# Attention of a hybrid decoder layer on one core: all tokens ahead of the expert gather, or the second half of the tokens between its slots

## Time and profile before

| | us |
|---|---|
| median of 3 runs | 3849.35 (3846.76 to 3849.93) |
| the profiled execution | 3843.72 |
| its span, first to last instruction | 3841.9 |
| mean granted TensorE clock | 0.953 |
| first slot's product (DVE, line 1436) starts | 1045.9 |
| last slot's product starts | 3825.2 |

### The profile page before, as it was taken

One profiled execution on the slowest core, in us unless ns is written; L12 is line 12 of the kernel. 1 busy time (PEld: TensorE's weight loads), 2 busy tenths in 40 slices (PEclk: granted clock), 3 DMA queues, 4 the chain that ended last, 5 costly groups with the idle time before them and its releaser, 6 DMA issues.

```text
span 3841.9 us, 34099 instructions
## 1 busy us (share of the span) xinstructions
PE 3173.3 (83%) x9592; PEld 1711.9 (45%) x9592; DVE 2383.7 (62%) x5856; ACT 1312.8 (34%) x3737; POOL 1447.5 (38%) x1288
## 2 busy tenths in 40 slices
PE   7888886698899799978897889998777777777776
PEld 5767665577444355534443444443222222222222
DVE  4555555314366687767766676666666667667664
ACT  2333333322133345543333233333333333333332
POOL 2122210241044456545544344333444444344442
PEclk9989896899899999999998999999999999999999
DMA  2000000521599999999999899999999999999997
GB/s 84 17 23 22 22 11 4 226 75 65 186 409 421 418 393 413 420 407 408 406 388 398 337 387 420 420 421 421 417 420 416 414 415 417 416 413 414 418 418 328
DMA packets 190464, 1203.34 MB, mean 313 GB/s; under 512 B 21840, under 2 KB 30032, under 8 KB 58704
## 3 DMA queue, kind: packets, MB, share of 16 engines
q0 software_dynamic: 147456, 1073.81, 68.1%
q1 hardware_dynamic: 42112, 127.43, 8.9%
q10 hardware_dynamic: 720, 0.13, 0.0%
HBM read 1180.31 MB, written 20.97 MB: 313 GB/s over the span
## 4 chain that ended last, share of the span: by engine, by line
DMA 28%; PE 23%; DVE 7%; ACT 3%; issue 3%; POOL 1%; POOLq 0%; DVEq 0%
DMA ring<-uv,idx 27%; PE r_o L1600 18%; DVE ring L1436 5%; PE w_ps L1475 3%; PE w_ps L1586 1%; ACT diag L1128 1%; ACT gel L1118 1%; ACT coef L1122 0%; POOL ring L953 0%; ACT L1103 0%; DMA y_scr<-zn 0%; DVE wo L1244 0%; DVE gates L1240 0%; PE w_ps L1569 0%; DVE yn_e L1414 0%
## 5 line engine op out<-in xcount | busy, mean ns | idle before, releaser
L1600 PE MATMUL r_o<-ring,diag 128*128 128x512 f32 x4096 | 1958.6, 613 | 456.7 <-ACT diag L1128 456.2
L953 POOL DMA_INDIRECT ring<-uv,idx x1024 | 1147.7, 1121 | 1614.0 <-PE r_o L1600 1513.6
L1436 DVE CUSTOM_DVE_ANT_0 ring<-ring,ytok 128x1024 f32<-128x1024 f32 x1024 | 1295.3, 1266 | 681.4 <-DMA ring<-uv,idx 680.3
L1600 PEld LDWEIGHTS r_o<-ring,diag 128*128 128x128 f32 x4096 | 762.4, 193 | 1463.5 <-ACT diag L1128 730.8
L1118 ACT ACTIVATE gel<-dot 128x2 f32<-128x2 f32 x512 | 104.1, 203 | 1695.6 <-DVE dot L1436 1694.7
L1128 ACT ACTIVATE diag<-ident,coef 128x128 f32<-128x128 f32 x1024 | 348.0, 387 | 3.2 <-PE r_o L1600 3.1
L1475 PE MATMUL w_ps<-xh,wb 128*128 128x512 f32 x640 | 270.9, 473 | 37.6 <-POOL wb L926 37.2
L67 PE MATMUL j_ps<-xT_hi,wa 128*128 128x512 f32 x768 | 258.6, 409 | 18.6 <-DVE xT_lo L355 18.6
L1586 PE MATMUL w_ps<-yT,wq 128*128 128x512 f32 x512 | 257.0, 604 | 5.2 <-DMA wq<-wq 4.5
L1122 ACT ACTIVATE coef<-gel,gate 128x1 f32<-128x1 f32 x1024 | 245.9, 287 | 16.8
L250 POOL TENSOR_SCALAR st_a<-st_a 128x1 f32<-128x1 f32 x64 | 12.2, 191 | 489.5 <-ACT sq L305 489.5
(11 more groups left out here) (162 smaller groups left out, 3014.5 us busy)
## 6 DMA issues: line engine op xcount, KB each, us to landing
wb_raw<-w_in SPq DMA_DIRECT2D x40, 512.0 KB, 7.7
wq<-wq SPq DMA_DIRECT2D x32, 512.0 KB, 7.9
ring<-uv,idx POOLq DMA_INDIRECT x1024, 13.0
wa_raw<-w_in SPq DMA_DIRECT2D x24, 512.0 KB, 3.3
wc_raw<-w_branch SPq DMA_DIRECT2D x16, 768.0 KB, 8.6
wo_raw<-w_out SPq DMA_DIRECT2D x16, 512.0 KB, 15.7
s_scr<-s_out SPq DMA_DIRECT2D x16, 512.0 KB, 9.6
s<-s_scr SPq DMA_DIRECT2D x64, 128.0 KB, 10.3
```

Source lines behind the costliest of these rows:

```text
L953: nc.gpsimd.indirect_dma_start(out=ring[t % RING][:], out_offset=None, in_=a["uv"], in_offset=bass.IndirectOffsetOnAxis(ap=idx[:, slot:slo ...
L1436: nc.vector.tensor_tensor_reduce(ring[r][:, 0:D], ring[r][:, 0:D], ytok[n % 2][:], 1.0, 0.0, ALU.mult, ALU.add, dot[:, slot:slot + 1]).the ...
L1600: ins = nc.tensor.matmul(o_ps[n % 2][half][:], diag[t % DIAGS][:], ring[t % RING][:, D + half * HALF:D + (half + 1) * HALF], start=slot == ...
```

## The change

Both blocks become one, `build`. Everything now runs by halves of the tokens, attention included.

- Half 0 (`stage(0)`, `BASES[0] = -4000`): 44 units (4 pooling, 8 each of q, k and v, 16 gates) of 512 tokens as before in three float32r matmuls, then 32 attention steps in plain float32. k and v of this half are stored in DRAM (`k_scr`, `v_scr`).
- Half 1 (`stage(1)`, `BASES[1] = 57`): 44 units, 32 attention steps against the keys of both halves, branch products and `w_out`, all in plain float32 and with no split. The gates of this half are stored in `g_scr` as they are made and loaded again after the attention. k and v of half 0 come back per head.
- In the gather nothing changes. `by_vector` always returns False, so `PE_SUMS[t]` is `t + 1`.

The slot numbers, and the order on each engine within `stage(g)`:

```diff
-BASES = (-4000, 72)
-UNIT_LEN = 6; BRANCH_LEN = 13; NORM_LEN = 12; HEAD_LEN = 16
+SEQ = [("p", i) for i in range(NP)] + [(r, 0) for r in "qkv"]
+for _h in range(H):
+    SEQ += ([(r, _h + 1) for r in "qkv"] if _h + 1 < H else []) + [("g", 2 * _h), ("g", 2 * _h + 1)]
+BASES = (-4000, 57)
+LAND = 12
+STEP = 6
+NSTEP = H * GT
+T_U = LAND
+T_A = T_U + 4 * (NP + 3) + 2
+T_B, BRANCH_LEN = T_A + 205, 9
+T_N, NORM_LEN = T_B + BRANCH_LEN * DC + 3, 12
+HEAD_LEN = (14, 16)
+SCORES_AT = (-69, 443)
+DO_LOGIT = (1, 1)
+DO_EXP = (3, 5)
+DO_MIX = (5, 6)
+DO_TURN = (8, 7)
+DO_VALUES = (11, 11)
+DO_OSB = (12, 12)
+DO_SQUARE = (13, 13)
+DO_ROOT = (15, 15)
+DO_ON = (17, 17)
+DO_OT = (22, 22)
+def unit_at(g, i):
+    if i < NP + 3:
+        return BASES[g] + T_U + 4 * i
+    i -= NP + 3
+    head, j = (i // 5, i % 5) if i < 5 * (H - 1) else (H - 1, i - 5 * (H - 1) + 5)
+    return BASES[g] + T_A + GT * STEP * head + (0, 4, 8, 14, 18, 2, 6)[j]
+def step_at(g, k):
+    return BASES[g] + T_A + STEP * k
+def merged(*streams):
...
+        head = min(live, key=lambda item: item[0])
+        yield head[0]
+        head[0] = next(head[1], None)
```

`stage(g)` is now `merged(...)` of separate streams; of equal slot numbers the earlier stream goes first. On PE the streams are units, pooling, scores, turns, values, outs, rest:

```diff
+        def units(g):
...
+                for c in range(DC):
+                    yield unit_at(g, i) + c // 3
...
+                        ins = nc.tensor.matmul(bank[:], w_raw[1][i % 3][:, c, :], x_raw[1][:, c, :], start=c == 0,
+                                               stop=c == DC - 1)
+        def scores(g):
...
+                for c in range(g + 1):
+                    yield step_at(g, k) + 2 * c
...
+                    if i >= 2:
+                        pe.wait_ge(logit_done, i)
+                    source = k_own[g][h % 2] if c == g else k_old[h % 2]
+                    for wh in range(2):
+                        rows = slice(wh * DH, (wh + 1) * DH)
+                        nc.tensor.matmul(score_bank(g, wh)[:, 0:n], q[g][h % 2][rows, qs], source[rows, 0:n], start=True,
+                                         stop=True).then_inc(s_ready, 1)
+        def turns(g):
...
+                    yield step_at(g, k) + DO_TURN[g] + 2 * c
+        def values(g):
...
+                yield step_at(g, k) + DO_VALUES[g]
+        def outs(g):
...
+                yield step_at(g, k) + DO_OT[g]
```

On DVE (streams pooling, logits, outputs, transposed, rest), and the exponentials on ACT:

```diff
+        def logits(g):
...
+                for c in range(g + 1):
...
+                    for wh in range(2):
...
+                        yield step_at(g, k) + DO_LOGIT[g] + (2 * c + wh if g else 0)
...
+                        dve.wait_ge(s_ready, i + 1)
...
+                yield step_at(g, k) + DO_MIX[g]
...
+                dve.wait_ge(e_ready, 2 * m + 2)
+        def outputs(g):
...
+                yield step_at(g, k) + DO_OSB[g]
+                dve.wait_ge(o_done, m + 1)
...
+        def transposed(g):
...
+                yield step_at(g, k) + DO_OT[g] + 1
+                dve.wait_ge(on_turned, m + 1)
...
+        def exponents(g):
...
+                yield step_at(g, k) + DO_EXP[g]
+                act.wait_ge(mx_ready, m + 1)
+                for wh in range(2):
+                    nc.scalar.activation(e[g][k % 2][:, wh, 0:n], e[g][k % 2][:, wh, 0:n], ACT.Exp,
+                                         bias=nmx[:, wh:wh + 1], accum_out=den[:, wh:wh + 1]).then_inc(e_ready, 1)
```

More of the change, by code:

```diff
@@ L43 @@
 KB = 1024
[L46 to L53, removed]
-BASE = 16512
[L59 to L70, removed]
@@ L76 @@
[L76 to L97, removed]
@@ L100 @@
[L100 to L117, removed]
@@ L812, in stage @@
[L812 to L820 removed]
+                for c in range(2):
+                    load_branch(0, c)
+                sp.dma_start(gb[:, 0], a["ln2_g"].to_broadcast([P, D])).then_inc(gb_in, 16)
@@ new lines, in rest @@
+            sp.wait_ge(unit, UNITS * (g + 1))
+            if g:
+                for r in range(2):
+                    sp.wait_ge(gate_saved[r], 16 * NGATE // 2)
+                for half in range(2):
+                    sp.dma_start(gates[1][:, DC * half:DC * (half + 1)],
+                                 g_scr[DC * half:DC * (half + 1)].rearrange("j p w -> p j w")).then_inc(gate_back, 16)
+                load_branch(1, 1)
+                yield step_at(g, NSTEP - 1) + DO_ON[g] + 2
+                sp.wait_ge(on_ready, NSTEP * (g + 1))
@@ L821, in stage @@
+            load_out(g)
             for n in range(2, DC):
@@ L867, in stage @@
             store_scores(RH - 1)
+        def stage(g):
+            if g == 0:
+                return merged(units(0), keys_out(), rest(0))
+            return merged(rest(1), units(1), gate_stores(), keys_back())
         def search_in(k):
@@ L938, in stage @@
                 nc.gpsimd.tensor_tensor(rstd1, var1, mhalf1, ALU.pow).then_inc(rstd1_ready, 1)
+        def stage(g):
+            if g == 0:
+                return merged(units(0), roots(0), rest(0))
+            return merged(roots(1), rest(1))
         def root(n):
@@ L1034, in stage @@
[L1034 to L1042 removed]
+                yield unit_at(g, i) + 3
+                act.wait_ge(unit, UNITS * g + i + 1)
@@ L1054, in turned @@
+                nc.scalar.activation(mt_of(n)[0][:], gates[0][:, 0:DC, n * P:(n + 1) * P], ACT.Copy).then_inc(m_hi, 1)
             def turned(n):
@@ new lines, in units, with pooling @@
+                ins.then_inc(unit, 1)
+                if SEQ[i][0] == "v":
+                    yield unit_at(g, i) + 4
+                    pe.wait_ge(evac, u + 1)
+                    if i == NP + 2 and g == 0:
+                        pe.wait_ge(consts, 5)
+                    for b in range(GT):
+                        ins = nc.tensor.transpose(bank[:, b * P:(b + 1) * P], vT[g][:, b * P:(b + 1) * P], ident[:])
+                    ins.then_inc(v_turned, 1)
+        def pooling(g):
+            for i in range(NP):
+                b = NP * g + i
+                yield unit_at(g, i) + (7 if g else 9)
+                bank = ps[2 + b % 2]
@@ new lines, in outs @@
+        def outs(g):
+            for k in range(NSTEP):
+                m = NSTEP * g + k
+                yield step_at(g, k) + DO_OT[g]
+                pe.wait_ge(on_ready, m + 1)
+                if g == 0 and k:
+                    pe.wait_ge(o_ready, m)
+                if g:
+                    behind = min(k + 3, NSTEP - 1)
+                    pe.wait_ge(logit_done, score_no(1, behind, 1, 1) + 1)
+                nc.tensor.transpose(out_bank(g)[:, 0:P], on[:], ident[:]).then_inc(on_turned, 1)
@@ L1590, in stage @@
                         compare(hp - 1)
-            yield score_at(g, RH) + 8
+            yield score_at(g, RH) + part
             compare(HP * (g + 1) - 1)
+        def stage(g):
+            return merged(units(g), pooling(g), scores(g), turns(g), values(g), outs(g), rest(g))
         def spread(n, slot):
             t = SLOTS * n + slot
-            pe.wait_ge(diag_ready, t + 1)
+            u = PE_SUMS[t]
+            pe.wait_ge(diag_ready, u)
             if slot == 0 and n >= 2:
```

1384 lines of the change are left out of this document (663 added, 721 removed).

## The result

The changed kernel takes **4101.6 us** (median of 4, 4094.0 to 4104.4) against 3848.1 of the kernel before on the same chip (4 runs, 3845.1 to 3849.9): ratio **1.0656, 95% interval 1.0638 to 1.0675**. It is slower, as forecast, but by 254 us instead of 117, and outside the range. The execution profiled took 4094.0 us (span 4092.2), 0.2% under the median.

A forecast was written before the change was run, and what follows sets the result against it. PE, busy 83% of the span, was held to stand waiting for diagonals when DVE waits between slots. 566 to the first product + 2314 outside the steps + 1084 in them = 3964, 3966 with the surround; range 3860 to 4060.

The forecast's parts named there:

- Three VectorE waits a step: Steps, slots 99 to 291: DVE waits for PE at one slot's distance three times a step, for logits twice and the copy.
- the clock: Steps: after a wait PE runs at the lower clock level; 1.2 us for each of 32 steps, 38 us.
- Part 2: Gather slots outside the steps, with half 1's units, branch and norm between them, plus the end: 2314 us.
- The new DMA traffic: Gather: some 24 MB more, 57 us at 420 GB/s, costs nothing because slots 69 to 376 take over 2.9 us.
- The forecast's own sign of being wrong: Wrong if slots 99 to 291 take under 5 us each, or the first product is later than 620 us.
- Part 1: Ahead of the gather: half 0's attention, branch at 353 us, first product at 566 us instead of 1046, -480.
- the forecast's lower bound for the first product: Ahead of the gather: first product at 535 us if PE runs without gaps.
- Part 3: The 32 steps among slots 99 to 291: 1084 us, 5.6 a slot; bounds 706 and 1150.
- The scores: Steps: score matmuls of 64 rows run side by side, 0.86 us a pair of 512 columns; other bound 1.72.
- The mechanism's fine print: Steps: each DVE wait stands ahead of a pair's second product, so PE stands for the rest of the round.
- The first rival: Steps: PE is the bound and the waits are covered, 706 instead of 1084 us, total 3588; chance 12%.
- Its condition: Steps: the result is faster than before once they need under about 955 us.

The follow-up runs named there:

- e11: Single-slot kernel (GROUP 1, 3826 us) with first three weight blocks loaded earlier and GpSimd's first two branch splits earlier: 8 us less; first product 630.5 against 628.0.
- e10: Changed kernel, pairs kept, VectorE's waits for TensorE and the mix in second-half steps at two slots, transposed output in the values' bank: 3725 us.
- e1: Changed kernel with the second half's stage begun one slot later (BASES 58 for 57), shifting step parity against the pairs: 29 us less.
- e12: The two-slot kernel with pairs (3725 us), only the logits put back to one slot behind their scores: +163 us.
- e14: The two-slot kernel with pairs (3725 us), only the mix put back to one slot behind the exponentials: +66 us.
- e15: The two-slot kernel with pairs (3725 us), only the copy of the transposed output put back to one slot behind its transpose: +55 us.
- e2: Changed kernel with ScalarE making gel, coefficient and diagonal slot by slot instead of in pairs (GROUP 1 for 2): 3826 us, 276 us less.
- e3: Changed kernel with the gather's Gelu replaced by Exp (output differs), removing 73 of 105 table loads in the steps' stretch: 26 us less.

## Why the prediction was right and wrong

**Right: the sign and its reason.** The gain ahead of the gather is given away in the steps, because VectorE waits inside its queue of products and TensorE then stands for diagonals. Three VectorE waits a step, the clock after them, slots 443 on at the old rates: as forecast. Part 2 was forecast at 2314 us with its end and took 2311 (4092.2 - 629.6 - 1151.6). That it fits to 3 us is in part luck: the branch took 16 more and the norm tiles 17 less than forecast. The new DMA traffic cost nothing visible: slots 57 to 99 took 141 us for 145 forecast.

**Wrong: two terms, 64 and 68 us.** Less the 3 us of part 2 they make the 128 us by which the profiled execution (4094.0) missed the forecast; the median lies another 8 above it. The forecast's own sign of being wrong, a first product later than 620 us, came up; the other, under 5 us a slot in the steps, did not (6.0).

*Part 1, the first product at 566 us; it was 629.6.* The step that failed is the 334 us from the start to the branch (19 to 353), which took to 414. I priced TensorE there at 289 us of work, 317 with gaps, by the matmul rate at full clock of the window of 50 us in the earlier trace rows. It was busy 337 us at a granted clock of 0.92 and stood for 62. So the price in busy time was 48 low, and about 13 lay in standing. About half of the 48 is the clock: TensorE was busy at the lower level for 42 us of this stretch, and its first 17 records, before 30 us, follow one another every 0.43 us instead of 0.23; together I estimate 25 us. The other 23 were priced too low at full clock: the units' records take some 0.24 us and not 0.225, the steps 1.8 us each and not 1.6, and the pooling's 3 us were not in the sum. I had the row that says so: the old attention also ran at 0.88 and was busy 555 us where my prices gave 430, and I took the pure rate. The way from branch to first product was right (213 forecast, 215). Nor were the gaps that I could name in the trace worth anything on the first product (e11). What binds the start behind them stays open. (By its own terms the forecast's lower bound for the first product is 538 us, not 535.)

*Part 3, the steps, 1084 us; they were 1152.* e10 gives the parts: 742 us is what TensorE needs for these slots at a granted clock of 1.00, 877 what it took, 275 it stood:

```
            work at full clock   lower clock   standing   sum
forecast          706                 38          340     1084
measured          742                135          275     1152
```

The standing was put too high by 65 us; perhaps a head's projection matmuls hide more of the round than I let them, but no run shows it. The work was 36 low, by e10 at 1.77 us a slot for my 1.72 and 4.1 a step for 3.7. The largest miss is **the clock, 97 us**: "with such a wait in every step I add 1.2 x 32 = 38" counts it once a step, and at the price of one slot. The groups of sums in the steps, after and in e10, show the rest:

```profile
L1584 PE MATMUL r_o<-ring,diag 128*128 128x512 f32 x784 | 476.9, 741 | 274.5 <-ACT diag L869 274.5
```

```profile
L1585 PE MATMUL r_o<-ring,diag 128*128 128x512 f32 x781 | 372.7, 600 | 34.8 <-ACT diag L873 34.6
```

104 of the 135 us are in the slots' sums, the very records that follow a wait. Their four starts lie over 1.5 us from first to last in 83 of the 192 slots, against none in e10; 67 of the 83 are slots that waited themselves, and the other 16 the second of such a pair. The granted clock stood at the lower level in 70 stretches of the steps. Each began in one of the 92 waits or at most 1.4 us after it, and the 256 us for which TensorE was busy in them, at half speed, account for 128 of the 135. A wait of 2.6 us could be enough (1399.02 above); it need not be the 4.59 of the earlier trace rows. But 22 of the 92 waits, 2.6 to 3.1 us long, brought no such stretch. The Trainium skill (TensorE: Matmul & The Clock Gate, HAM oscillation — how this bites in real kernels) describes a loop whose TensorE waits in every pass and starts every pass at the low level. This trace agrees in the main, with waits for VectorE and ScalarE: 70 of the 92 waits for diagonals brought the low level, and the granted clock of the steps is 0.88. I read the rows for one such pass and did not multiply by the waits that I had listed myself.

**The scores** do run side by side, as I took it. Four records of 64 rows and 512 keys in float32 follow as two pairs:

```profile
1369.90 1.13 PE L1408 MATMUL w_ps<-kold,q 64*128 64x512 f32 x4
```

The price of 0.86 us was a little low: in e10, at full clock, the next record starts 1.06 us after such a pair's first (1211.33 to 1212.39), against the other bound of 1.72.

**The mechanism's fine print** was wrong in one point: the place "ahead of a pair's second product". e1 shows that the parity hardly matters. What matters is that only one slot lies between TensorE's matmul, or ScalarE's exponentials, and VectorE's use of it (e12, e14, e15), and that the pairs lengthen the way back (e2).

**The first rival** (the waits are covered, 3588 us) is what e10 makes real: its steps take 777 us, not 706, and with the start as it was the whole is 3725. Its condition was sound: under 955 us in the steps the change wins. With the 416 us that the start really gave (1045.9 to 629.6) in place of 480, and part 2 as it was, the point lies near 894 by the same sum; e12 with 936 is slower than the kernel before (1.0113), e14 with 837 faster (0.9859).

## What to carry to other kernels

Where a stage is woven into another one's slots, count for each cross-engine wait how many slots lie between the producer's instruction and the consumer's, and try two where there is one. One slot costs 1.7 to 2.5 us a wait here, and a placing with the same matmuls and vector instructions was worth 9% (e10 against the changed kernel). Take away all the short waits before judging any: the copy gave 100 us, all the others but the logits nothing more, and the whole 376. And when TensorE stands in every pass, price the lower clock once for every wait, not once for every pass: 92 waits at my price of 1.2 us would have made 110 of the 135 us.

## What the hardware showed that I had not expected

- The lower clock level costs half as much as the standing that brings it on: 135 us of slower matmuls to 275 us idle. It came after waits as short as 2.6 us, though not after each, and never in the steps of e10, whose longest wait for a diagonal was 1.7 us.
- A table load between Gelu and Exp takes 1.28 us of ScalarE, but taking 73 of 105 out of the stretch of the 32 steps gave only 20 us (e3), 0.27 us a load.
- ScalarE at single slots has 49 us more to do in the steps (e2: 448 for 400 us), and it hardly costs anything: in the placing with two slots (453 for 400) single slots lose 9 us there to the pairs, and win 23 in the whole.
